# Decoder step on one Trainium2 core: sample queries through DRAM, sample scores between the softmax steps

## The reference, cut to what matters

```python
qn = rms_norm(q, q_norm) * (HEAD_DIM ** -0.5)
kn = rms_norm(ka, k_norm)
...
    s = jnp.einsum('bshd,bsjhd->bshj', q, kg) - slopes[None, None, :, None] * offs...
    lse = jax.nn.logsumexp(s, axis=-1)
    p = jnp.exp(s - lse[..., None])
    return jnp.einsum('bshj,bsjhd->bshd', p, vg), lse
...
outs = [dilated_gather_attention(qn, k_ext, v_ext, slopes, w, d, buf) for w, d in DIL_PATTERNS]
mix_w = jax.nn.softmax(lse_stack, axis=0)
```

## Time and profile before

| what | value |
|---|---|
| median of three runs | 1532.42 us (1518.5 to 1537.64) |
| the profiled execution | 1525.86 us |
| its span, first to last instruction | 1524.1 us |
| stage B in the span | 844 to 1343 us |
| middle pairs, pair 6, last pair | about 62.4, 52 and 72 us |

### The profile page before, as it was taken

How to read it: one execution, slowest core, us unless ns; L and a number is a source line. 1 busy time by engine, 2 the same in 40 slices (tenths; PEclk the granted TensorE clock), 3 DMA queues, 4 the chain that set the end, 5 groups by cost and what they waited for, 6 DMA issues and landing times.

```text
span 1524.1 us, 33729 instructions
## 1 busy us (share of the span) xinstructions
PE 1453.1 (95%) x14669; PEld 1359.4 (89%) x14669; DVE 744.7 (49%) x1437; ACT 518.8 (34%) x856; POOL 454.9 (30%) x239
## 2 busy tenths in 40 slices
PE   4999999999999999999999999999999998799998
PEld 4998989989899998989989988989989887689998
DVE  3226574753857556474753546355363464500000
ACT  5333242412514233242412444444434354222221
POOL 0232121311212122121311423333334233933342
PEclk9999999998999999999998999999999999899999
DMA  6232130312204032130311753635636447244452
GB/s 203 70 85 60 36 102 15 106 30 64 74 14 115 22 79 64 40 98 15 105 43 38 196 132 84 164 95 140 134 93 154 105 112 202 78 126 123 128 152 58
DMA packets 251921, 143.05 MB, mean 94 GB/s; under 512 B 12078, under 2 KB 244847, under 8 KB 251247
## 3 DMA queue, kind: packets, MB, share of 16 engines
q1 hardware_dynamic: 228156, 125.90, 31.7%
q10 hardware_dynamic: 23618, 15.00, 3.3%
HBM read 125.36 MB, written 15.45 MB: 92 GB/s over the span
## 4 chain that ended last, share of the span: by engine, by line
PE 83%; DVE 8%; ACT 4%; issue 2%; DMA 2%; POOL 1%; SPq 0%; DVEq 0%; ACTq 0%; POOLq 0%
PE acc L460 55%; PE head_banks L876 3%; PE head_banks L866 3%; PE head_banks L881 2%; PE head_banks L818 2%; DVE AREN L1530 1%; PE head_banks L1019 1%; PE head_banks L1039 1%; DVE AREN L1760 1%; PE head_banks L1032 1%; DVE AREN L1543 1%; PE head_banks L988 1%; PE head_banks L917 1%; PE head_banks L926 1%; PE head_banks L1066 1%
## 5 line engine op out<-in xcount | busy, mean ns | idle before, releaser
L444 POOL TENSOR_TENSOR WL<-WR,WH 128x1024 fp32r<-128x1024 f32 (+1 forms) x164 | 396.2, 2416 | 991.0 <-ACT WH L436 988.3
L460 PE MATMUL acc<-XH,WH 128*128 128x260 f32 (+1 forms) x2624 | 576.9, 301 | 4.9 <-POOL WL L444 4.3
L460 PE MATMUL acc<-XH,WL 128*128 128x260 f32 (+1 forms) x2624 | 530.8, 284 | 0.0
L460 PE MATMUL acc<-XL,WH 128*128 128x260 f32 (+1 forms) x2624 | 530.3, 284 | 0.0
L460 PEld LDWEIGHTS acc<-XH,WH 128*128 128x128 f32 (+1 forms) x2624 | 406.6, 190 | 40.2 <-issue 26.9
L460 PEld LDWEIGHTS acc<-XL,WH 128*128 128x128 f32 (+1 forms) x2624 | 406.7, 189 | 0.0
L460 PEld LDWEIGHTS acc<-XH,WL 128*128 128x128 f32 (+1 forms) x2624 | 406.3, 189 | 0.0
L436 ACT ACTIVATE WH<-WR 128x1024 fp32r<-128x1024 f32 (+1 forms) x164 | 171.9, 1048 | 180.4 <-PE acc L460 172.8
L468 ACT ACTIVATE AREN<-acc 128x520 f32<-128x520 f32 (+1 forms) x82 | 49.2, 600 | 188.3 <-PE acc L460 188.1
L1811 DVE TENSOR_TENSOR AREN<-head_banks,AREN 128x512 f32<-128x512 f32 x16 | 11.1, 691 | 170.0 <-PE head_banks L1090 170.0
L1760 DVE CUSTOM_DVE_ANT_0 AREN<-AREN 128x128 f32<-128x128 f32 (+3 forms) x64 | 62.2, 972 | 16.5 <-ACT AREN L1365 16.5
(11 more groups left out here) (229 smaller groups left out, 1669.4 us busy)
## 6 DMA issues: line engine op xcount, KB each, us to landing
WR<-in_w_in SPq DMA_DIRECT2D x128, 512.0 KB, 4.0
WR<-in_w_out SPq DMA_DIRECT2D x32, 512.0 KB, 6.2
out<-AREN ACTq DMA_DIRECT2D x32, 256.0 KB, 3.4
AREN<-in_cache_k_win SPq DMA_DIRECT2D x16, 384.0 KB, 8.5
AREN<-in_cache_v_win SPq DMA_DIRECT2D x16, 384.0 KB, 9.2
mix_scratch<-AREN ACTq DMA_DIRECT2D x16, 260.0 KB, 4.9
AREN<-in_x_prompt SPq DMA_DIRECT2D x4, 1024.0 KB, 7.9
AREN<-in_cache_k_win SPq DMA_DIRECT2D x8, 512.0 KB, 7.1
```

The source lines that it names most:

```text
L444: pool.tensor_tensor(WL[:, k % 2, :, 0:M], WR[:, k % 4, :, 0:M], WH[:, k % 2, :, 0:M].bitcast(F32), ALU.subtract).then_inc(s_lo, 1)
L460: mm = pe.matmul(acc[0:M, hf, 0:HT], w[:, k % 2, j, 0:M], x[:, kt, hf * HT:(hf + 1) * HT], start=(kt == 0 and n == 0), stop=(kt == KT - 1 ...
```

## The change: the query's way and the place of the samples' scores

The transposes `qb` and their entry in every table go. Instead ScalarE, behind its work for `tokv` and `stok`, waits for QN and writes the 128 x 8 sample queries to a DRAM scratch as its first DMA of the pair; behind its six other issues it waits for that write and issues a read that broadcasts the 4 KB to all 128 partitions (QB8, 512 KB in SBUF). VectorE waits before QN until the write of the pair before has landed.

`score(0)` waits for QN and for the copy of the values out of bank 1, no more for `pr2`. The six operations of the samples' scores (`pr0`, `rd0`, `pr1`, `rd1`, `pr2`, `rd2`) stand one each behind softmax steps 0 to 5 on VectorE, after `mx` of step j + 2. The product reads QB8 by sample and feature, which is a step of 8 floats, since QB8 lies by feature and sample. The unit tables are dealt anew.

```diff
-BEHIND_B = {"ssum": 6, "tokv": 2, "stok": 2, "qb": 13,
-            **{f"s{b}": (4, 2, 2, 2)[b] for b in range(QB)},
-            **{f"t{j}": (2, 1, 2, 1, 2, 1, 3, 1)[j] for j in range(len(JS))},
-            "o3": 1, "sct": 4, "pwt": 3, "av": 2}
+BEHIND_B = {"ssum": 6, "tokv": 2, "stok": 4,
+            **{f"s{b}": (5, 3, 2, 2)[b] for b in range(QB)},
+            **{f"t{j}": (3, 2, 3, 2, 3, 2, 4, 1)[j] for j in range(len(JS))},
+            "o3": 2, "sct": 5, "pwt": 3, "av": 2}
...
-BEHIND_SHORT = {"ssum": 5, "tokv": 1, "stok": 1, "qb": 12, **{f"s{b}": (3, 1, 1, 1)[b] for b in range(QB)},
-                **{f"t{j}": (1, 1, 1, 1, 2, 1, 2, 1)[j] for j in range(len(JS))}, "o3": 1, "sct": 4, "pwt": 3, "av": 2}
-BEHIND_OWN = {"ssum": range(OWN, OWN + 6), "qb": range(OWN + 6, UNITS)}
+BEHIND_SHORT = {"ssum": 5, "tokv": 2, "stok": 3, **{f"s{b}": (4, 2, 1, 1)[b] for b in range(QB)},
+                **{f"t{j}": (2, 1, 2, 1, 2, 2, 3, 1)[j] for j in range(len(JS))}, "o3": 1, "sct": 5, "pwt": 3, "av": 2}
+BEHIND_OWN = {"ssum": range(OWN, OWN + 7), "tokv": range(OWN + 7, OWN + 10), "stok": range(OWN + 10, UNITS)}
...
+    q_d = nc.dram_tensor("query_scratch", (PAIRS, 128, NB), F32, kind="Internal").ap()
...
+        QB8 = ba.take(128, NB)
...
-                pe.wait_ge(b_dve, DVE_B.at(i, "qn"))
-                pe.wait_ge(b_act, ACT_B.at(i, "tokv"))
-                for b in range(NB):
-                    mm = pe.transpose(HB[:, b // 4, 128 * (b % 4):128 * (b % 4 + 1)],
-                                      QN[:, T + b:T + b + 1].to_broadcast([128, 128]), ident)
-                mm.then_inc(b_pe, PE_B.one("qb"))
-                fill("qb")
-
                 def score(b):
                     n = 128 * (b + 1)
-                    pe.wait_ge(b_dve, DVE_B.at(i, f"mx{2 * b - 1}" if b else "pr2"))
+                    if b == 0:
+                        pe.wait_ge(b_act, ACT_B.at(i, "tokv"))
+                    pe.wait_ge(b_dve, DVE_B.at(i, f"mx{2 * b - 1}" if b else "qn"))
...
+                act.wait_ge(b_dve, DVE_B.at(i, "qn"))
+                act.dma_start(q_d[i], QN[:, T:TT]).then_inc(o_q, 16)
                 act.dma_start(KC[96:97, 1, :, :], SKV[0:NB, 0, :]).then_inc(s_krow, 16)
...
-                feed("qb")
+                act.wait_ge(o_q, 16 * (i + 1))
+                act.dma_start(QB8.rearrange("p c b -> p (c b)"),
+                              q_d[i].rearrange("c b -> (c b)").unsqueeze(0).to_broadcast([128, 128 * NB])).then_inc(s_q, 16)
...
-                dve.wait_ge(b_pe, PE_B.at(i, "qb"))
-                dve.wait_ge(s_kc, (i + 1) * 48)
-                dve.wait_ge(s_krow, done(1, i, 16))
-                for t, n in enumerate(TS):
-                    if t:
-                        after(f"rd{t - 1}")
-                    dve.tensor_tensor(PR[0:n, :, :].rearrange("p b c -> p (b c)"),
-                                      KC[0:n, t, :, :].rearrange("p b c -> p (b c)"), HBF[0:n, 0:NB * 128], ALU.mult)\
-                       .then_inc(b_dve, DVE_B.one(f"pr{t}"))
...
+                def sample_scores(j):
+
+                    t, n = j // 2, TS[j // 2]
+                    if j == 0:
+                        dve.wait_ge(s_q, 16 * (i + 1))
+                        dve.wait_ge(s_kc, (i + 1) * 48)
+                        dve.wait_ge(s_krow, done(1, i, 16))
+                    if j % 2 == 0:
+                        if t:
+                            after(f"rd{t - 1}")
+                        dve.tensor_tensor(PR[0:n, :, :], KC[0:n, t, :, :], QB8[0:n, :, :].rearrange("p c b -> p b c"),
+                                          ALU.mult).then_inc(b_dve, DVE_B.one(f"pr{t}"))
+                    else:
+                        after(f"pr{t}")
+                        dve.tensor_reduce(SCO[0:n, t, :], PR[0:n, :, :].rearrange("p b (h d) -> p (b h) d", h=2),
+                                          mybir.AxisListType.X, ALU.add).then_inc(b_dve, DVE_B.one(f"rd{t}"))
...
                     if j + 2 < nj:
                         largest(j + 2)
+                    if j < 6:
+                        sample_scores(j)
```

More of the change, by code:

```diff
@@ L241, in build @@
         BIAS = sb("BIAS", [128, 3])
-        ARENA_N = 26000
+        ARENA_N = 26100
         AREN = sb("AREN", [128, ARENA_N])
@@ L274, in build @@
         o_vec, s_rv = sem("sample_vectors_out"), sem("sample_vectors_landed")
+        o_q, s_q = sem("queries_out"), sem("queries_landed")
         s_sst, o_sst = sem("sample_state_landed"), sem("sample_state_out")
@@ L397, in build @@
         two_on = lambda s, j: [f"{s}{j + 2}"] if j + 2 < nj else []
+        sample_of = lambda j: [f"{'rd' if j % 2 else 'pr'}{j // 2}"] if j < 6 else []
         seq = ["s0"] + [x for b in range(QB) for x in ([f"s{b + 1}"] if b + 1 < QB else [])
                         + [f"t{2 * b}", f"t{2 * b + 1}", f"o{b}"]]
-        PE_B = Steps(["ssum", "tokk", "tokv", "stok", "qb", *seq, "sct", "pwt", "av", "avt"])
+        PE_B = Steps(["ssum", "tokk", "tokv", "stok", *seq, "sct", "pwt", "av", "avt"])
         ACT_B = Steps(["ln", "rn", "tokk", "tokv", "stok", "sgg", "ex0", "ex1",
@@ L403, in build @@
         DVE_B = Steps(["kn", "qn", "sl",
-                       *[x for t in range(3) for x in (f"pr{t}", f"rd{t}")],
-                       "mx0", "mx1", *[x for j in range(nj) for x in [f"pm{j}", f"rz{j}", f"pn{j}"] + two_on("mx", j)],
+                       "mx0", "mx1",
+                       *[x for j in range(nj) for x in [f"pm{j}", f"rz{j}", f"pn{j}"] + two_on("mx", j) + sample_of(j)],
                        "gate", "smx", "spm", "srz", "spn", "mixp", "mixs"])
@@ L1716, in pair_b @@
                                          op0=ALU.mult, op1=ALU.mult).then_inc(b_dve, DVE_B.one("kn"))
+                if i:
+                    dve.wait_ge(o_q, 16 * i)
                 dve.scalar_tensor_tensor(out=QN, in0=ZB[:, 0, :], scalar=QW[:, 0:1], in1=RNB[:, 0, :],
@@ L1722, in pair_b @@
                    .then_inc(b_dve, DVE_B.one("sl"))
-                dve.wait_ge(b_pe, PE_B.at(i, "qb"))
-                dve.wait_ge(s_kc, (i + 1) * 48)
-                dve.wait_ge(s_krow, done(1, i, 16))
-                for t, n in enumerate(TS):
-                    if t:
-                        after(f"rd{t - 1}")
-                    dve.tensor_tensor(PR[0:n, :, :].rearrange("p b c -> p (b c)"),
-                                      KC[0:n, t, :, :].rearrange("p b c -> p (b c)"), HBF[0:n, 0:NB * 128], ALU.mult)\
-                       .then_inc(b_dve, DVE_B.one(f"pr{t}"))
-                    after(f"pr{t}")
-                    dve.tensor_reduce(SCO[0:n, t, :], PR[0:n, :, :].rearrange("p b (h d) -> p (b h) d", h=2),
-                                      mybir.AxisListType.X, ALU.add).then_inc(b_dve, DVE_B.one(f"rd{t}"))
+                def sample_scores(j):
[13 more added lines that the diff above has]
+                                          mybir.AxisListType.X, ALU.add).then_inc(b_dve, DVE_B.one(f"rd{t}"))
                 def largest(j):
```

## The result

The change made the kernel slower: 1573.86 us in the median of four runs (1563.51 to 1577.99), beside 1529.14 for the kernel before on the same chip, a ratio of 1.030 with a 95% interval of 1.025 to 1.034. The profiled execution took 1570.86 us, 45 more than the one that the prediction was summed on. The forecast, 1557, had the direction and most of the mechanism: 32 of the 45 us were forecast, all in stage B, and most of the rest sits in the first, the seventh and the last pair.

A forecast was written before the change was run, and what follows sets the result against it. TensorE, busy 95% of the span, was taken as the bound: time falls only if it works or waits less. 1525.9 + 18.6 - 1.1 + 8.6 + 6 = 1558, stated as 1557 us; own range 1543 to 1570, overall 1528 to 1574.

The forecast's parts named there:

- The product, 2.0 us: VectorE's samples' products in stage B: reading queries with a step of 8 floats makes each take 2.0 us.
- The rival of a free step: Stage B products take 1.25 us because the step of 8 floats costs nothing; total 1542 us, chance 0.2.
- The meetings with GpSimd: Stage B: VectorE stands until GpSimd's 2.4 us weight-remainder operation ends; a product meeting one loses 0 to 2.4 us.
- The middle pair, +3.1: Six full stage B pairs: waits of 4.4 us against 0.5, less 0.8 for transposes; +3.1 each, bounds -1.3 and +4.5.
- cover holds: Middle pairs, t1 to t6: products fit in VectorE's idle time and larger entries, no wait left; 1521 us, chance 0.13.
- Pair 0, +2.0: First stage B pair: a middle pair's +3.1, with 1.1 us given back since its first score waits for QN; +2.0.
- Pair 6, +8.6: Stage B pair with only 48 units: waits 9.0 us against 1.3, less 0.8, plus 1.7 for clock; bounds +2 and +11.
- I count 1.7 once: Pair 6: 1.7 us lost to TensorE's lower granted clock after a wait, counted a single time.
- The last pair, +6: Last stage B pair: ScalarE's DMAs queue behind its evacuation, t0 +2.5, then +3.5 behind it; bounds 0 and +12.
- unless the write is slower: Middle pair, ScalarE: waiting for the query's 4 KB write costs nothing, as 3.7 us pass before the read's issue.
- the chain behind t0: Last pair: six operations, at least 7.5 us, enter; about 7 us of waits for slow TensorE steps absorb most; +3.5.
- The late query: Write and read take 8 us instead of 4.5, costing some 2 us more in seven pairs: +14, 1571 us, chance 0.12.

The follow-up runs named there:

- after: The kernel with the change described, against the kernel before it: 1573.86 us median, ratio 1.0296.
- without the step: Changed kernel with products reading the broadcast queries in the order they lie, so the samples' outputs change; ratio to the kernel before the change 1.0155.
- the quarters: Changed kernel with each stage B weight remainder formed by GpSimd in four operations of 256 columns, not one of 1024; ratio to the kernel before the change 1.0227.
- the run with one query: Changed kernel where only pair 0 writes and reads its queries and the other seven pairs multiply by those; ratio to the kernel before the change 1.0241.
- one sample of eight: Changed kernel whose six samples' operations take one sample instead of eight in pairs 1 to 7; ratio to the kernel before the change 1.0078.
- all together: Changed kernel with queries as rows, earlier query write and read, GpSimd remainders in four, last pair's units and gate moved; ratio to the kernel before the change 1.0044.
- the queries by rows: Changed kernel with queries transposed once, copied with the samples' keys and values, and written as rows, all results kept; ratio to the kernel before the change 1.0149.

## Why the prediction was right and wrong, point by point

- **The product, 2.0 us: right.** Shortest 2001 ns in after, 1219 without the step. The price taken from the one strided reduction of before (0.77 ns an element) measured 0.76. The rival of a free step falls. The Trainium skill (Advanced Engine Details and Errata, SBUF Cachelines) has the penalty without a price; this is the price here, for fp32 with a step of 32 bytes.
- **The meetings with GpSimd: right.** In a middle pair all three products took more than 2.0 us, and in pair 2 the first ended 1.97 us behind the remainder that it met. The Trainium skill (SBUF — State Buffer, Who interferes with whom) calls the shared port pair an exclusive lock, held by whichever starts first for its whole instruction; the quarters agree, in both directions. What the forecast left out is that a product that comes first pushes the remainder onto a later operation, as the run with one query shows.
- **The middle pair, +3.1: right** in the sum and in its places (1.55, 0.78, 1.58 and 0.26 us of waits at t1, t3, t5 and t6; forecast 1.3 to 1.7, 0.6, 1.6, 0.6). The transposes' 0.8 is not measured by itself: outside its waits the pair fell by 0.5 us, and the two kernels whose TensorE never waits there differ by 1.0. The rival "cover holds" falls with it.
- **Pair 0, +2.0: too low by 2.3.** The step that failed is the landing of the query: a write of at most 3.7 us and 4.5 for the read, as in a middle pair. Here they took 6.1 and 6.3, beside SP's weight and cache loads; VectorE stood 3.7 us for the query, the first product met no remainder, TensorE waited 3.3, and the granted clock went to 0.79, some 1.4 us of slow work.
- **Pair 6, +8.6: too low by 4.2.** The waits were 9.7 us where I had 9.0, though not all in their places: 5.8 at t1 as forecast (5.5), but then one of 3.4 where the remainder held the normalisation, not three short ones. The mis-sized term is "I count 1.7 once" for the clock: two waits of 5.8 and 3.4 us were each followed by a stretch at 0.50, 5.8 us of slow work.
- **The last pair, +6: too low by 4.0.** ScalarE's order was as described, the evacuation at +14.7 (forecast +14.5). Two steps failed. The first is the wait for the query's write, put at nothing "unless the write is slower" in the middle pair and left out here: the write took 5.1 us, ScalarE stood 1.5 for it, and t0 moved by 3.5, not 2.5. The second, and larger, is the chain behind t0, taken at +3.5 because slow TensorE steps would absorb most of the operations: it grew by 6.5. With one sample of eight that part was 5.5 us shorter, so the operations' length is nearly all of it. The absorbing was argued, and didn't happen.
- **The late query** was among the rivals at 1571, near the measured time, but for the wrong reason: I let it cost 2 us in seven pairs. In the middle pairs it is worth 0.2 to 0.7 us, because a query in time only moves the meeting on to the operations behind the product; it bites in pairs 0, 6 and 7. Against it I had set that a rush of loads stands in the last pair only. It stands in the first as well, and in pair 6, where write and read took 3.3 and 5.4 us, no rush is needed: the pair has few units, and the product stood 3.37 us for its query.
- **The size.** Forecast were 32 us; the three odd pairs added 10.5, the later start and the end 2.1. I gave 0.30 to a loss of more than 2%; the loss is 3.0%, and these pairs carried it there.

What the new route of the queries does without the new place of the scores, or the other way round, is not shown: the prompt's scores can't come earlier while the queries lie in the banks that they need.

## What to carry to other kernels

Price an operand's step before its route: laying the eight queries out by rows gave back half of the loss. Moving work into the gaps of a dependent chain costs its full length wherever the other engine has no more units to spare, and a long wait can cost again in the clock (here after 3.3, 3.4 and 5.8 us); so sum a pair with few units apart from the full ones. When a DMA goes from one queue's end back to its start (write, wait, read), look at what else is being loaded at that moment, and at what stands behind the wait on the issuing engine.

## What was not expected of the hardware

- The hold between VectorE and GpSimd goes by who comes first. With GpSimd's operation cut in four, the four took 4.81 us instead of 2.80 beside a product, and VectorE lost 0.2 instead of 1.0. With the query in time and GpSimd's operation whole, that operation took 4.38 instead of 2.39, and the normalisation behind the product 2.07 instead of 0.29.
- 4 KB to DRAM took 3.4 us in a middle pair, 6.1 in the first and 5.1 to 6.3 in the last, as 128 pieces of 32 bytes beside SP's loads of caches, weights and mixed rows. As 8 rows of 512 bytes it took some 6.6 us in the last pair of all together, and at most 3.7 in that of the queries by rows (write issued 14.8 us after the first sums, read 18.6). The traffic showed; what the form is worth is open.
- In after, waits of 1.6 us left the granted clock at 1.00; behind those of 3.3, 3.4 and 5.8 us it was 0.50 to 0.79 in the next stretches. The length of the wait alone doesn't settle it: without the step, one of 2.09 us in the first pair was followed by 0.59, and one of 3.18 in the last by 1.00.
